# The trial value's update in a top-k search: from a three-operand to a two-operand VectorE instruction

## What is computed

```
score = einsum('bqh,bqhs->bqs', w * idx_scale, relu(einsum('bqhd,bsd->bqhs', qi, ki)))
score = where(visible, score, -inf)
_, idx = top_k(score, 256)            # per query: the 256 best keys
p = softmax(logits over the kept keys);  ya = p @ v
y = concat(ya * silu(ga), yb * silu(gb)) @ W_out
x = layer_norm(ALPHA * x + y)
```

## Time and profile before

| what | value |
|---|---|
| median of 3 runs | 1628.86 us (1627.3 to 1629.36) |
| the profiled execution, its time | 1628.88 us |
| the profiled execution, its span | 1627.0 us |
| PE busy | 1459.7 us, 90% of the span |
| DVE busy | 1272.8 us, 78% |
| ACT busy | 915.7 us, 56% |
| POOL busy | 413.7 us, 25% |
| chain that ended last, by engine | PE 66%, DVE 17%, issue 8%, ACT 4%, POOL 3%, DMA 1% |
| L1439, all 224 | 345.7 us |
| L1446, all 224 | 93.0 us, mean 415 ns |
| L1443, all 224 | 34.5 us, mean 154 ns |
| PE's mean granted clock | 0.934 of full speed |

### The profile page before, as it was taken

How to read it: one execution, slowest core, us unless ns; L and a number is a source line. 1 busy time by engine, 2 the same in 40 slices (tenths; PEclk the granted TensorE clock), 3 DMA queues, 4 the chain that set the end, 5 groups by cost and what they waited for, 6 DMA issues and landing times.

```text
span 1627.0 us, 19213 instructions
## 1 busy us (share of the span) xinstructions
PE 1459.7 (90%) x6469; PEld 1064.1 (65%) x6520; DVE 1272.8 (78%) x2297; ACT 915.7 (56%) x1769; POOL 413.7 (25%) x268
## 2 busy tenths in 40 slices
PE   7999999999999768758978978998999899989997
PEld 6887877877887545545556635665656565468886
DVE  3578879988988779889999899988997762028776
ACT  3584846845853798526878734876873433311110
POOL 3314325533314433102221210112120511002221
PEclk9999999999999779779998889997998879999999
DMA  6332223422225433212131220222113311024442
GB/s 235 89 99 97 101 79 118 142 91 65 83 73 139 125 89 79 50 33 75 39 78 46 67 63 1 57 56 69 31 45 108 110 61 44 14 71 155 149 136 91
DMA packets 104305, 136.34 MB, mean 84 GB/s; under 512 B 6498, under 2 KB 81126, under 8 KB 103950
## 3 DMA queue, kind: packets, MB, share of 16 engines
q1 hardware_dynamic: 91344, 93.16, 21.0%
q10 hardware_dynamic: 9216, 31.20, 4.9%
q0 software_dynamic: 3648, 10.76, 2.2%
HBM read 92.76 MB, written 42.34 MB: 83 GB/s over the span
## 4 chain that ended last, share of the span: by engine, by line
PE 66%; DVE 17%; issue 8%; ACT 4%; POOL 3%; DMA 1%; SPq 0%; DVEq 0%; POOLq 0%; ACTq 0%
PE psum L1155 24%; PE psum L1344 9%; PE psum L1298 8%; DVE above L1439 4%; PE psum L1226 3%; PE psum L1286 3%; PE psum L1287 2%; PE psum L1186 2%; PE psum L1171 2%; PE psum L1260 2%; PE psum L1259 2%; PE psum L1285 2%; PE psum L1188 2%; DVE junk L1531 2%; DVE lb L1507 1%
## 5 line engine op out<-in xcount | busy, mean ns | idle before, releaser
L1439 DVE TENSOR_SCALAR_CACHE_REDUCE above<-dist,trial 128x512 bf16<-128x512 int32 (+13 forms) x224 | 345.7, 1543 | 5.7
L999 ACT ACTIVATE above<-dist,trial 128x384 bf16<-128x384 int32 (+13 forms) x224 | 280.7, 1253 | 44.1 <-DVE trial L1412 21.2
L1155 PE MATMUL psum<-x_hi,w_hi 128*128 128x512 f32 x640 | 254.7, 398 | 24.1 <-POOL w_lo L822 11.3
L1298 PE MATMUL psum<-prob,vw 128*65 128x512 f32 x544 | 266.9, 593 | 2.1 <-ACT out_a L949 1.5
L1094 ACT ACTIVATE prob<-psum 128x512 f32<-128x512 f32 x272 | 158.5, 593 | 186.5 <-PE psum L1298 144.7
L1155 PE MATMUL psum<-x_lo,w_hi 128*128 128x512 f32 x640 | 252.6, 395 | 0.0
L1155 PE MATMUL psum<-x_hi,w_lo 128*128 128x512 f32 x640 | 252.3, 394 | 0.0
L1531 DVE CUSTOM_DVE_ANT_0 junk<-psum,mask 128x512 bf16<-128x512 f32 (+3 forms) x320 | 184.5, 607 | 34.0 <-PE psum L1226 19.3
L1226 PE MATMUL psum<-ka_ext,qa_ext 128*128 128x512 f32 (+3 forms) x320 | 139.9, 487 | 52.1 <-DVE part_max L1531 38.9
L1286 PE MATMUL psum<-qa_mix,ka_mix 128*128 128x512 f32 x272 | 167.9, 617 | 2.2 <-DVE qa_ext L1552 1.4
L1155 PEld LDWEIGHTS psum<-x_hi,w_hi 128*128 128x128 f32 x640 | 122.2, 191 | 53.2 <-POOL w_lo L822 14.4
(11 more groups left out here) (156 smaller groups left out, 2874.3 us busy)
## 6 DMA issues: line engine op xcount, KB each, us to landing
raw<-w_tiles SPq DMA_DIRECT2D x40, 512.0 KB, 4.1
proj<-staged ACTq DMA_DIRECT2D x40, 512.0 KB, 3.2
qb_raw<-proj SPq DMA_DIRECT2D x32, 256.0 KB, 4.2
qa_raw<-proj SPq DMA_DIRECT2D x32, 256.0 KB, 4.5
yt_raw<-y_t SPq DMA_DIRECT2D x16, 512.0 KB, 5.3
x_row<-x_res SPq DMA_DIRECT2D x16, 512.0 KB, 4.0
out<-z ACTq DMA_DIRECT2D x16, 512.0 KB, 2.6
x_raw<-xT SPq DMA_DIRECT2D x12, 512.0 KB, 4.6
```

The lines of the kernel that those rows point to most:

```text
L999: nc.scalar.activation(above[:, 0, 0:n], src, ACT.Sign, scale=-1.0, bias=u, accum_out=count[:, 0:1]).then_inc(sign_counted, 1)
L1155: last = pe.matmul(psum[:, 2 * u + m, :], wt[:, u, k, :], xt[:, k, 512 * m:512 * m + 512], start=(k == 0 and q == 0), stop=(k == KT - 1 an ...
L1298: pe.matmul(psum[0:65, 6 + g, :], vw[:, kt, 0:65], prob[:, u % 3, :], start=(kt == 0), stop=(kt == b)).then_inc(a_used, 1)
L1439: v.tensor_scalar(above[:, 1, 0:n], src, u, None, ALU.is_ge, ALU.add, accum_out=count[:, 1:2]).then_inc(own_counted, 1)
```

## The change

In DVE's search step the instruction that moves the trial value is replaced. The old one, scalar_tensor_tensor, computes `(accept * 2^(31-i)) + u`, with `accept` and `u` as its two tensor inputs. The new one, tensor_scalar, computes the same with `accept` as its only tensor input: the power of two is its first number (an immediate), and `u` is its second, read from SBUF as a per-partition scalar. `u` is still the output too. Semaphores, order and all else are as they were; ACT's search isn't touched.

```diff
                 dve.wait_ge(own_accepted, done["count"])
-                v.scalar_tensor_tensor(u, accept[:, 1:2], 2.0 ** (31 - i), u, ALU.mult, ALU.add) \
+                v.tensor_scalar(u, accept[:, 1:2], 2.0 ** (31 - i), u, ALU.mult, ALU.add) \
                     .then_inc(own_moved, 1)
```

## The result

The changed kernel takes 1616.47 us (median of 10 runs, 1612.23 to 1619.76), the kernel before 1625.44 in the same rounds (10 runs, 1620.2 to 1629.36). The ratio is 0.994 with a 95% interval of 0.9925 to 0.9955, so 9 to 10 us are gained. The prediction had 3.4 us and 1625.5. The profiled executions are 1628.88 and 1619.76 us (spans 1627.0 and 1617.9).

What follows compares the result with a forecast made beforehand. It took PE to bound the projection and an alternating PE-DVE chain the attention stretch; 4.8 us from holds less 1.4 for the pointer, net 3.4 off 1628.88, gave 1625.5 us, likeliest 1622.5 to 1627, 8-in-10 range 1619 to 1632.

Steps and rivals of the forecast that it cites:

- still held: DVE's move: the new form waits for POOL like the old, leaving only the pointer's cost: 1630.3 us; chance 0.06.
- The projection: Projection stretch: DVE's 47.9 us of tail worth nothing directly; shifted collisions from -4 to +4 us, taken as 0.
- The holds on the chain: Attention stretch: eight held moves, 8.0 us on the chain, of which 4.8 us gained after cuts by what is late next.
- 1218.49: Held move at this time (us) in attention: PE had waited 2.17 us behind it, so all of 1.67 us counts.
- 649.62: Held move at this time (us) in attention: PE had waited long enough behind it, so all of 1.17 us counts.
- 802.64: Held move at this time (us) in attention: PE had waited 2.50 us behind it, so all of 0.88 us counts.
- 914.31: Held move at this time (us) in attention: PE waited only 0.48 us behind it, so 0.48 us counts.
- The pointer: 28 moves on attention's chain: reading `u` by pointer costs 0.05 us more each, 1.4 us lost.
- The base: Whole kernel: the forecast starts from the profiled execution's 1628.88 us, taken as the median to 0.02.
- More gained than the chain shows: Attention's 9.2 us of DVE tail, with some us in the projection, could shift as a whole: 1618.3 us; chance 0.12.
- Given back: DVE reaches other two-input instructions, above all L1516 and L1518, during splits; half or all gain goes: 1627 to 1629; chance 0.20.
- slower by new collisions: DVE, coming earlier, meets POOL's splits at L1518, 2.07 us a time; four more beyond two give 1633.8 us; chance 0.17.

Runs made afterwards that it cites:

- the run with two elements: Changed kernel with its move made over two adjacent elements, of which one is used: 1628.12 us, ratio 1.0005 to the kernel before.
- the eight: Kernel before with the new form only in eight search steps whose moves were held on the chain: 1612.3 us (0.9908), again 1613.06 us (0.9914).
- the five others: Kernel before with the new form in thirteen steps, adding five attention moves held over 0.3 us to the eight: 1615.74 us, ratio 0.9919.
- the seven: Kernel before with the new form in the eight steps except the next to last of the last search: 1620.98 us, ratio 0.9965.
- the delay: Changed kernel with an extra 1.63 us DVE count before the move in the last search's next to last step: 1623.06 us, ratio 0.9979.
- one new: Kernel before with the new form only in the next to last step of the last search: 1620.11 us, ratio 0.9954.
- two pointers: Changed kernel with two more numbers read by pointer in L1443, the decision before the move: 1625.32 us, ratio 0.9986 to the kernel before.

## Why the prediction was wrong, and where it was right

**The new instruction.** Predicted 211 ns, never held; measured 213/214/219. DVE's busy time fell by 45.2 us where 46 were predicted. The rival "still held" is refuted by it, and the run with two elements shows how near it was.

**The projection.** Predicted nothing; the run with the new form there alone gave 1.0003, and the wait for ACT's half took up the gain as predicted. PE's idle time is 17.6 us for 16.3.

**The holds on the chain.** The choice of places was right: the eight steps alone give all the gain and more, the five others nothing. Of the lengths, the two largest were right: PE's wait behind 1218.49 lost 1.56 us of the 1.67 predicted, that behind 649.62 lost 1.13 of 1.17. That behind 802.64 lost 0.62 of 0.88, and that behind 914.31 none of its 0.48.

**The step that failed is the price of a hold.** The sum "0.54 + 1.17 + 0.88 + 0.1 + 0.48 + 1.67 = 4.8 us" takes each at its length, cut by what is late next. It has no term for TensorE's clock behind PE's wait. The 1.67 measured 7.5 us alone and 7.9 on top of the seven; the other 3.1 measured 5.7. So 4.8 should have been 13 to 15. For the one at 1218.49 that the rest is the clock's is shown, by the delay and by the time over the same work with the clock at either level, and with the base below it comes to about the whole miss of 9.0 us: some 6 too little here, 3.4 too much in the base. For the seven it is not shown: no run takes one of them alone. The runs with the seven new have a mean clock of 0.940, those of the kernel before in the same rounds 0.936, which fits a share of the clock, but doesn't say where.

The rows for it were in the trace of before: the granted clock of 0.89 in the attention stretch means that a fifth of it ran at 1.2 GHz, and the earlier trace rows had the wait of 2.17 us. I read the clock as a property of the stage and didn't ask what PE had done before it fell.

**The pointer.** Predicted 28 x 0.05 = 1.4 us. The changed kernel, with the pointer in all steps, gains 10.3 us, the eight 14.0 and 15.0: some 4 us more for the same holds removed. The term was perhaps three times too small, but the intervals (each some 1.4 to 2.2 per mille wide on either side) leave 1.4 us possible. The mean clocks differ too, 0.941 against 0.945 and 0.946, and by the spread between executions below that alone goes with some 4 us. How much of the difference is the pointer's stays open.

**The base.** The sum started from 1628.88 us. In the ten runs of the comparison the kernel before has 1625.44 as its median and 1629.36 as its highest; the execution that was profiled lies near the top of its spread. Of the 9.0 us between 1625.5 and 1616.47, 3.4 are this.

**The rivals.** "More gained than the chain shows" came nearest (1618.3), for a reason that didn't occur: nothing came from the projection or from holds off the chain. "Given back" and "slower by new collisions" weren't seen: L1516 sums to 9.71 us where it had 9.63, L1518 to 12.94 in both. Behind 1079.80 and 1106.87 the hold did pass on to L1516 (1.10 and 1.05 us, from 0.55 and 0.57), as the 0 in the sum had it. The rival miscounts one thing: L1518 takes some 2.2 us three times in the 14 of the attention stretch, and five times in all 16, not three.

## What to carry to other kernels

When a short wait of TensorE is removed or added, look at the granted clock of the microseconds behind it before pricing it at its length: here 1.6 us at one place were worth 6 to 8, and for the same 1.6 us where DVE had slack no loss was measured. A one-element instruction on DVE with two tensors from SBUF, or a two-element one with one, can stand still for the whole of a GpSimd instruction; put what TensorE waits for ahead of it in the order, or give it one element and a pointer, and do so at the few places on the chain, since the pointer costs 0.06 us everywhere.

## What the runs showed of the hardware that was not expected

**The clock behind a wait.** At one place in 18 traces, waits of 2.16 to 2.20 us were followed by 0.57 or 0.72 over 12 us, waits of 1.39 and 1.62 us by 0.72, waits of 0.53 to 0.62 us by 1.00. It isn't the wait alone. At the second place 14 traces have a wait of 1.78 to 1.84 us: the clock behind it is 0.57 in ten, 0.72 in two and 1.00 in two (one new, two pointers). From there to the third L1259 it took 38.5 us with 0.57 (changed) and 34.5 with 1.00 (one new). At the third, PE waits 0.24 or 0.25 us in all 18, and the clock is 0.50 to 0.62. What decides it these runs don't show.

**Clock and spread.** Over the 79 runs of the kernel before beside the experiments, times and mean clocks go together (correlation -0.86), 1.0 us for each 0.001. By rounds, the correlation is -0.85 (23 runs), -0.94 (26), -0.91 (13), and only -0.36 (17). In the 23, the mean clock is 0.935; that of the changed kernel's 6 runs is 0.941, that of the eight's 0.946 and 0.945. A single trace can be several us off by this: the run with the new form in the projection alone, which is the kernel before in attention, has its first L1259 at 1215.92, 5.2 us ahead of before, with the same wait of 2.17 us.

**The hold.** One tensor from SBUF and one element: never held, in 224 instances of L1443 in each kernel and 224 of the new move (219 ns at the longest), though some 60 of each in the trace after start inside a split or cast of POOL. Two elements: held up to 2.46 us. Unheld, the two take 214 and 229 ns.
